# Index scores, turned rows and the mask moved beside the projection slabs of a two-layer decoder step

## The chip, the cores and the metric

The program runs on one core of one Trainium2 chip. The metric is the device time of one execution in microseconds (us), from launch to end, on that core. In the rows PE is TensorE's matmul side, PEld its weight loads, ACT ScalarE, DVE VectorE, POOL GpSimd, SP SyncE (it only issues transfers here); "ACTq" and "SPq" are the transfers that those engines issue.

## The reference, cut to what matters

One step of a decoder with two layers over 256 prompt tokens and 8 sample tokens (264 columns), width 2048, all in f32. Layer 0 picks keys with an indexer, layer 1 uses a forget gate. Both also attend into 256 memory tokens, and both end in a mixture of experts.

```python
# layer 0
q, k, v, qi, ki, wi, qm = split(h @ w_in)          # qi: 16 index heads of 64, ki: one index key
s = einsum('qhd,ld->qlh', qi, ki) * 64 ** -0.5
score = einsum('qlh,qh->ql', relu(s), wi * 16 ** -0.5)
sel = top_k(where(pos_k <= pos_q, score, -1e30), topk)   # prompt: 64 of 256; sample: 256 of 2049
# attention with ALiBi over the selected keys only
# layer 1
q, k, v, f, qm = split(h @ w_in)
c = cumsum(concat(cached log f, log_sigmoid(f + b_f)))   # bias c_q - c_k on the scores
# both layers
mk, mv = mem @ w_mem_kv                            # 256 memory tokens, 4 heads
mix = concat(self attention, memory attention) @ w_o
h = LN(alpha * h + mix); h = LN(alpha * h + moe(h))
```

The keys, values, index keys and forget gates of the sample tokens' past (8 sequences x 16 pages x 128 tokens) lie in pages that are found through a page table. New keys and values, memory keys and values, index keys and gates are outputs too.

## The kernel before, in words

Activations stand with the feature on the partition: `X` holds 16 chunks of 128 x 264 (`Xc`), `AT` the same for the memory tokens (`Ac`). Weights pass through a ring of six 2 MB slots (`ring`). `plan` lists the ring's units of each layer in order, SP issues them in that order, and a unit waits until the slot's last user has left it (`free`). PE waits for a unit with `arrived` and gives it back with `leave`.

A **slab** (`slab`, matmuls on L620) is one projection of 512 output columns: two units of 2 MB, 2 halves x 4 blocks f x 8 chunks c, so 64 f32 matmuls of 128x128 by 264 columns (128 records in the trace, since each f32 matmul is recorded twice). It fills four of the eight PSUM banks, banks 4 to 7 and 0 to 3 in turn, and ACT copies them out (L1361). `slab` has a hook, `beside(x)`: it is called after each four matmuls, x from 0 to 15, and what it issues stands between the slab's matmuls in PE's order. Before the change only layer 1's gates use it (`gate_sums`, L752; `gate_rows`).

The order on PE up to the attention, each step starting when the last is through:

- Layer 0, start: constants, page table, `ln` rows, the ALiBi table (1 MB) and then x are loaded. `turn_rows(0, "x")` transposes x (L596 for the 256 prompt rows, L598 for the 8 sample rows), and ACT copies it to `X`.
- `indexer`: the projection to index keys and head weights (`kiwi`, L659 and L661), a few transposes of it, two slabs `qi`. Then 16 prompt index steps (L689: PE two matmuls, ACT two Relus on L1421, DVE two multiply-adds on L1819/L1821). Then the cached index keys: 16 pieces are turned (L728), copied by ACT, multiplied with the queries (`product`, L705), rectified (L1430) and summed over heads (`rows`, L715). DVE then finds the 256 largest of 2049 per sequence (`sample_topk`, 32 pairs on L1803/L1804, ends with `mask_ready`), after that the prompt's 64 of 256 (`prompt_topk`), then waits in `add_mask` (L1874).
- Slabs q (3), kv, qm. Then `natural` (L640) turns new keys and values back to token rows for the outputs; ACT copies and stores them.
- `memory`: `turn_rows(layer, "mem")` transposes the memory tokens (L596) into `Ac`, two slabs `mkv`, `natural` for memory keys and values.
- Layer 0 only: `mask_rows` (L784) spreads the mask over partitions for `add_mask`. ACT's `pad_queries` puts the queries into two zeroed tiles `Qz`, `Qmz`, which POOL clears once `memory_done` is given after ACT's stores. `sample_scores` turns cached keys (L807) and multiplies (L816).
- Layer 1 is the same without the indexer, with 3 q, 2 kv and 1 qm slab. `cached_gates` (L777) turns the cached gates after `natural`; they were loaded by ACT in 128 small transfers.

ACT issues the page loads of the cached index keys for six sequences (`load_ik`), three before each of the two `qi` slabs are copied; SP loads the other two into the ring unit `ik`.

After this come attention, the output projection (L1066), the experts (L1227, L1257, L1271), untouched here.

## Time and profile before

| | |
|---|---|
| median of 3 runs | 2381.66 us (2380.25 to 2386.26) |
| the profiled execution's own time | 2382.95 us |
| its span, first to last instruction | 2381.3 us |
| PE busy | 2212.7 us, 93% |
| DVE busy | 669.0 us, 28% |
| ACT busy | 492.4 us, 21% |
| read from HBM | 640.20 MB, 271 GB/s over the span |
| mean granted TensorE clock | 0.963 of full |

The share of PE is an average over stages. To read the profile for this change one looks at the stretches in which PE is less than fully busy or at its lower clock, in the 378 us before layer 0's cached keys and between 1192 and 1462 us for layer 1, and asks in each what ended the waits.

### The profile page before, as it was taken

How to read it: one execution, taken by the hardware profiler on the slowest of the kernel's cores; microseconds unless marked ns; L12 is line 12 of the kernel's file. 1: busy time of each engine (PE TensorE's matmuls, PEld its weight loads, DVE VectorE, ACT ScalarE, POOL GpSimd, SP SyncE). 2: the span in 40 equal slices, each digit the busy share in tenths (PEclk: the TensorE clock that was granted, in tenths of full speed). 3: DMA queues.
4: the chain of work that ended last, by engine and by line, in shares of the span. 5: the costliest groups of instructions: out<-in, count | busy, mean ns of one | idle time of the engine just before them, and what ended most of it. 6: DMA issues, size and time to landing. Idle time of an engine off the chain costs nothing.

```text
span 2381.3 us, 32060 instructions
## 1 busy us (share of the span) xinstructions
PE 2212.7 (93%) x12475; PEld 1388.5 (58%) x12475; DVE 669.0 (28%) x1226; ACT 492.4 (21%) x1112; POOL 4.2 (0%) x10
## 2 busy tenths in 40 slices
PE   6989999999999999999899998999999999998996
PEld 4768886577863434343377876644778443443433
DVE  0059940421283121222410010023015622222124
ACT  1130015530140101010220023742103311010114
POOL 0000000000000000000000000000000000000000
PEclk9999999999989999999999998998999999999998
DMA  8714356794329999999944444998632599999992
GB/s 264 220 66 147 141 156 206 234 319 176 118 88 428 389 430 402 429 402 422 380 155 125 160 165 153 361 339 302 246 142 107 210 427 402 429 394 428 385 429 108
DMA packets 210148, 647.88 MB, mean 272 GB/s; under 512 B 56841, under 2 KB 90266, under 8 KB 184154
## 3 DMA queue, kind: packets, MB, share of 16 engines
q1 hardware_dynamic: 174650, 636.32, 69.3%
q10 hardware_dynamic: 35376, 9.91, 1.8%
q8 instruction: 80, 1.31, 0.2%
q14 instruction: 42, 0.34, 0.0%
HBM read 640.20 MB, written 5.96 MB: 271 GB/s over the span
## 4 chain that ended last, share of the span: by engine, by line
PE 75%; DMA 13%; ACTq 4%; DVE 3%; ACT 3%; issue 2%; SPq 0%; DVEq 0%
PE bank L620 17%; PE bank L1227 12%; PE bank L1066 9%; DMA ring<-in_w_down 8%; PE bank L1257 7%; PE bank L1271 5%; DMA ring<-in_w_up 4%; PE bank L807 4%; PE bank L1212 4%; ACTq L395 3%; PE bank L816 2%; PE bank L947 2%; ACT arena L1361 2%; PE bank L928 1%; PE bank L1119 1%
## 5 line engine op out<-in xcount | busy, mean ns | idle before, releaser
L1227 PE MATMUL bank<-ring,AT 128*64 128x512 f32 x2048 | 451.6, 599 | 24.3 <-DMA ring<-in_w_up 21.9
L1361 ACT ACTIVATE arena<-bank 128x512 f32<-128x512 f32 (+2 forms) x530 | 260.8, 541 | 995.3 <-PE bank L620 357.7
L620 PE MATMUL bank<-X,ring 128*128 128x264 f32 x1664 | 377.6, 390 | 11.3 <-ACT X L1593 7.3
L620 PEld LDWEIGHTS bank<-X,ring 128*128 128x128 f32 x1664 | 319.4, 192 | 68.5 <-issue 8.6
L1227 PEld LDWEIGHTS bank<-ring,AT 128*64 128x64 f32 x2048 | 146.9, 138 | 319.3 <-issue 285.9
L1257 PE MATMUL bank<-ring,arena 128*64 128x512 f32 x1024 | 238.4, 622 | 42.3 <-DMA ring<-in_w_down 35.0
L1066 PE MATMUL bank<-AT,ring 128*128 128x264 f32 x1024 | 237.7, 395 | 7.1 <-DVEq L1952 7.1
L1066 PEld LDWEIGHTS bank<-AT,ring 128*128 128x128 f32 x1024 | 199.6, 196 | 43.2 <-issue 7.9
L2228 DVE TENSOR_TENSOR X<-bank,X 128x264 f32<-128x264 f32 x256 | 110.8, 433 | 331.0 <-PE bank L1271 328.1
L1257 PEld LDWEIGHTS bank<-ring,arena 128*64 128x64 f32 x1024 | 77.9, 143 | 192.5 <-issue 167.1
L1271 PE MATMUL bank<-arena 128*128 128x264 f32 x512 | 118.2, 389 | 0.0
L807 PEld LDWEIGHTS bank<-consts,ring 128*128 128x128 f32 x768 | 86.9, 146 | 49.4 <-ACT arena L1361 34.9
L1271 PEld LDWEIGHTS bank<-arena 128*128 128x128 f32 x512 | 96.0, 190 | 28.6 <-ACT arena L1361 13.0
L620 PE MATMUL bank<-AT,ring 128*128 128x256 f32 x512 | 110.9, 379 | 0.0
L807 PE MATMUL bank<-consts,ring 128*128 128x128 f32 x768 | 101.1, 287 | 7.0 <-issue 4.4
L620 PEld LDWEIGHTS bank<-AT,ring 128*128 128x128 f32 x512 | 97.1, 190 | 13.1
L1361 ACT ACTIVATE AT<-bank 128x512 f32<-128x512 f32 (+3 forms) x136 | 60.9, 481 | 173.9 <-PE bank L1212 166.6
L1803 DVE MAX8 arena<-arena 8x8 f32<-8x2049 f32 (+1 forms) x48 | 79.9, 1664 | 28.9 <-ACT arena L1361 27.3
L1212 PE MATMUL bank<-arena 128*128 128x256 bf16 x768 | 86.6, 273 | 0.0
L1212 PEld LDWEIGHTS bank<-arena 128*128 128x128 bf16 x768 | 73.8, 98 | 11.8 <-issue 3.4
L1804 DVE MATCH_REPLACE8 arena<-arena 8x2049 f32<-8x2049 f32 (+1 forms) x48 | 79.1, 1647 | 0.0
L1662 ACT ACTIVATE arena<-bank 128x512 f32<-128x512 f32 x16 | 9.6, 598 | 290.5 <-PE bank L1227 290.5
(326 smaller groups left out, 1433.7 us busy)
## 6 DMA issues: line engine op xcount, KB each, us to landing
ring<-in_w_gate SPq DMA_DIRECT2D x64, 2048.0 KB, 17.2
ring<-in_w_up SPq DMA_DIRECT2D x64, 2048.0 KB, 14.0
ring<-in_w_down SPq DMA_DIRECT2D x64, 2048.0 KB, 16.7
ring<-in_w_o SPq DMA_DIRECT2D x16, 2048.0 KB, 10.5
ring<-in_cache_b_k SPq DMA_DIRECT2D x128, 256.0 KB, 4.2
ring<-in_cache_b_v SPq DMA_DIRECT2D x128, 256.0 KB, 4.7
ring<-in_w_in_a SPq DMA_DIRECT2D x14, 2048.0 KB, 9.3
ring<-in_w_in_b SPq DMA_DIRECT2D x12, 2048.0 KB, 11.2
```

The source lines that it names most:

```text
L395: eng.dma_start(dst(g + k), cache[bass.ds(page, 1)].rearrange("a p w -> (a p) w")).then_inc(sem, 16)
L620: mm = pe.matmul(B[4 * (g % 2) + f][:, 0:n_tok], u[:, c * 512 + f * P:c * 512 + (f + 1) * P], src[8 * half + c][:, 0:n_tok], start=(half = ...
L807: mm = pe.transpose(B[(4, 5, 7)[m % 3]][:, pg * P:(pg + 1) * P], tile[:, x:x + P], ident)
L1066: mm = pe.matmul(B[bank0 + f][:, 0:T], u[:, c * 512 + f * P:c * 512 + (f + 1) * P], Ac[8 * half + c], start=(half == 0 and c == 0), stop=( ...
L1212: mm = pe.matmul(B[banks[g]][:, c * 2 * P:(c + 1) * 2 * P], M.part[t][k][:, at:at + P], M.sel[:, t * 2 * P:(t + 1) * 2 * P], start=False, ...
L1227: mm = pe.matmul(B[bank][64 * s:64 * s + 64, :], M.xsT[:, at:at + 64], ring[slots[s][0]][:, c * FE:(c + 1) * FE], start=(half == 0 and c = ...
L1257: mm = pe.matmul(B[2 + q][64 * s:64 * s + 64, :], M.hT[:, at:at + 64], ring[slots[s][0]][:, j * D + q * 512:j * D + (q + 1) * 512], start= ...
L1271: pe.matmul(B[2 + c % 4][:, 0:T], M.ys[:, c * P:(c + 1) * P], M.gt[a], start=True, stop=True).then_inc(sm("scattered"), 1)
L1361: return act.activation(out, in_, ACT.Copy, scale=scale)
L1803: link(dve.max(m8, sc))
L1804: link(dve.match_replace(sc, m8, sc, TAKEN))
L2228: dve.tensor_tensor(Xc[c], B[2 + c % 4][:, 0:T], Xc[c], ALU.add).then_inc(sm("scatter_added"), 1)
```

## The change

- **Start.** x is loaded first, in four units of 512 columns of each token row (`x` 0 to 3); the identity (the first 128 columns of the constants) and the sample rows come with the first. The page table follows, then `kiwi` in one transfer of 80 columns, then `ln` with the rest of the constants and the small biases. ALiBi comes with the unit `q` 3. `turn_x` turns the sample rows in 16 transposes and each prompt chunk in 2.
- **Index projection.** 16 matmuls with 80 output rows in place of 32 matmuls. Its transposes, the `ln` transpose and the head-weight product stand beside slab `qi` 0 (`turn_keys`).
- **Index scores.** Prompt steps 0 to 7 (heads of the first `qi` slab, order `INDEX_STEPS`) beside `qi` 1, steps 8 to 15 and the whole work on cached index keys beside q 0 (`index`).
- **Page loads.** ACT issues sequences 0 to 2 before the first `qi` slab is copied, 3 and 4 in pieces of four pages between the prompt steps; SP issues sequences 5 to 7.
- **Rows.** The memory unit comes ahead of the last kv slab, and its transposes stand beside that slab. Key and value rows and (layer 1) cached gates are turned beside qm, memory keys and the mask's spread beside `mkv` 1. Only the memory values' `natural` stands alone.
- **Queries.** POOL clears `Qz` early and ACT fills it right after the qm slab; `Qmz` (it shares its space with the memory values) is filled after the 12th turned piece of `sample_scores`.

The diff, cut to its core (ACT's, DVE's and POOL's sides follow the same order):

```diff
@@ plan
-        u += [("ln", 0, 5), ("x", 0, 1), ("xs", 0, 1), ("kiwi", 0, 2), ("qi", 0, 1), ("qi", 1, 1), ("qi", 2, 1),
-              ("qi", 3, 1), ("ik", 0, 16 * (NB - IK_EARLY))]
+        u += [("x", 0, 3), ("x", 1, 1), ("x", 2, 1), ("x", 3, 1), ("kiwi", 0, 1), ("ln", 0, 4)]
+        u += [("qi", k, 1) for k in range(4)] + [("ik", 0, 16 * (NB - IK_EARLY))]
...
-    u += [("q", k, 1) for k in range(6)]
-    u += [("kv", k, 1) for k in range(2 if layer == 0 else 4)]
-    u += [("qm", k, 1) for k in range(2)]
-    u += [("mem", 0, 1)] + [("mkv", k, 1) for k in range(4)]
+    u += [("q", k, 2 if layer == 0 and k == 3 else 1) for k in range(6)]
+    if layer == 1:
+        u += [("kv", k, 1) for k in range(2)]
+    u += [("mem", 0, 1)] + [("kv", 2 * layer + k, 1) for k in range(2)]
+    u += [("qm", k, 1) for k in range(2)] + [("mkv", k, 1) for k in range(4)]
@@ gpsimd
+                    pool.wait_ge(S("ix_rows_copied"), 5)
...
+                pool.memset(a.Qz, 0.0).then_inc(S("zeroed"), 1)
                 pool.wait_ge(S("memory_done"), layer + 1)
-                pool.memset(a.Qz, 0.0).then_inc(S("zeroed"), 1)
                 pool.memset(a.Qmz, 0.0).then_inc(S("zeroed"), 1)
@@ tensor
+            def turn_chunk(t, width, at, bank=0):
+                n = bump("rows_turned")
+                if n > 4:
+                    pe.wait_ge(S("rows_copied"), n - 4)
+                for g in range(2):
+                    mm = pe.transpose(B[bank + n % 4][:, g * P:(g + 1) * P], t[:, g * width + at:g * width + at + P], ident)
+                mm.then_inc(S("rows_turned"), 1)
...
+            def turn_memory(layer, x):
+                if x == 1:
+                    pe.wait_ge(S("slab_copied"), cnt["slab"] - 1)
+                    arrived(pe, layer, "mem")
+                if 1 <= x <= 8:
+                    t = ring[units[layer]["mem", 0][0]]
+                    for c in (2 * x - 2, 2 * x - 1):
+                        turn_chunk(t, D, c * P, 4)
...
+            def memory_rows(layer, a, x):
+                if x == 2:
+                    pe.wait_ge(S("slab_copied"), cnt["slab"] - 1)
+                if x in (2, 3):
+                    natural(a.memK, HM, x - 2, SEQ)
+                if layer == 0:
+                    if x == 5:
+                        pe.wait_ge(S("natural_copied"), cnt["natural"])
+                        pe.wait_ge(S("mask_ready"), 1)
+                    if 5 <= x <= 8:
+                        pe.matmul(B[x - 5][:, :], cst("to12", NB), a.S[0:NB, 512 * (x - 5):512 * (x - 4)], start=True, stop=True)\
+                          .then_inc(S("mask_rows"), 1)
+                    if x == 12:
+                        pe.wait_ge(S("mask_added"), 1)
...
@@ indexer
+                    if 1 <= x <= 4:
+                        prompt_step(6 + 2 * x, 0)
+                        prompt_step(7 + 2 * x, 2)
...
+                    if 6 <= x <= 12 and x % 2 == 0:
+                        product(x // 2 - 3)
+                    if x == 12:
+                        new_key()
+                    if 7 <= x <= 13 and x % 2:
+                        rows((x - 7) // 2)
+                    if x == 14:
+                        rows(4)
+                    if 4 <= x <= 11:
+                        turn_cached(2 * x - 8)
+                        turn_cached(2 * x - 7)
+
+                pe.wait_ge(S("ixp_relu"), 8)
+                slab(0, "q", 0, Xc, T, index)
                 pe.wait_ge(S("ix_rows_copied"), 5)
@@ layers
-                slab(layer, "qm", 0, Xc, T)
-                slabs_done()
-                natural(a.kT, a.nk, 3)
-                natural(a.vT, a.nk, 3)
-                if layer == 1:
-                    cached_gates(a)
-                pe.wait_ge(S("natural_copied"), cnt["natural"])
+                slab(layer, "kv", layer, Xc, T, lambda x: turn_memory(layer, x))
+                pe.wait_ge(S("rows_copied"), cnt["rows_turned"])
+                slab(layer, "qm", 0, Xc, T, lambda x: own_rows(layer, a, x))
                 memory(layer, a)
-                if layer == 0:
-                    mask_rows(a)
```

How the change moves instructions is plainest in PE's order in layer 0. Before, the cached index keys are a stage of their own ahead of the q slabs (L728 turns, L705 is the product, L715 the sum over heads):

```order
103 L705 MATMUL bank<-arena 32x512 [waits kt_copied]
104 L705 MATMUL bank<-arena 32x512 x3
105 L728 MATMUL bank<-consts,arena 64x128 [waits kt_copied]
106 L728 MATMUL bank<-consts,arena 64x128 x7
107 L728 MATMUL bank<-consts,arena 64x128 [waits kt_copied]
108 L728 MATMUL bank<-consts,arena 64x128 x7
109 L715 MATMUL bank<-arena 8x512 [waits ix_relu]
```

Nothing of a slab stands between these rows: each `kt_copied` is a wait on ACT's copy of a piece turned just before.

PE in the change, at x = 5 to 7 of slab q 0 (L642 is the slab, L768 turns, L778 is the product, L796 the sum over heads):

```order
103 L642 MATMUL bank<-X,ring 128x264 x4
104 L768 MATMUL bank<-consts,arena 64x128 [waits kt_copied]
105 L768 MATMUL bank<-consts,arena 64x128 x7
106 L768 MATMUL bank<-consts,ring 64x128 [waits kt_copied]
107 L768 MATMUL bank<-consts,ring 64x128 x7
108 L642 MATMUL bank<-X,ring 128x264 x4
109 L778 MATMUL bank<-arena 32x512 [waits ixp_relu,kt_copied]
110 L778 MATMUL bank<-arena 32x512 x3
111 L768 MATMUL bank<-consts,arena 64x128 [waits kt_copied]
112 L768 MATMUL bank<-consts,arena 64x128 x7
113 L768 MATMUL bank<-consts,arena 64x128 [waits kt_copied]
114 L768 MATMUL bank<-consts,arena 64x128 x7
115 L642 MATMUL bank<-X,ring 128x264 x4
116 L796 MATMUL bank<-arena 8x512 [waits ix_relu]
```

Four slab matmuls now stand between the steps of the chain, and the same waits on ACT's copies are kept.

PE in the change, in slab `mkv` 1 of layer 0 (L658 is `natural`, L691 the mask's spread). Before, the spread stood behind both `mkv` slabs:

```order
234 L642 MATMUL bank<-AT,ring 128x256 x11
235 L658 MATMUL bank<-consts,arena 128x128 [waits natural_copied,slab_copied]
236 L658 MATMUL bank<-consts,arena 128x128 x3
237 L642 MATMUL bank<-AT,ring 128x256 x4
238 L658 MATMUL bank<-consts,arena 128x128 [waits natural_copied]
239 L658 MATMUL bank<-consts,arena 128x128 x3
240 L642 MATMUL bank<-AT,ring 128x256 x8
241 L691 MATMUL bank<-arena,consts 128x512 [waits mask_ready,natural_copied]
242 L642 MATMUL bank<-AT,ring 128x256 x4
```

PE now meets the wait for `mask_ready` 24 matmuls into that slab, where before it met it after the slab and the `natural` of all memory rows.

## Rows read from the trace of the kernel before

**Rows 1.** Stretches: us, busy us of PE, PEld, DVE, ACT, POOL; granted clock, DMA share, GB/s.

```profile
0.00:33.00 33.00, 14.32 (x52) 8.34 (x53) 0.02 (x1) 7.82 (x18) 0.41 (x5) 1.00 0.91 298
109.00:128.00 19.00, 12.66 (x69) 5.98 (x68) 12.80 (x27) 11.80 (x40) 0.00 (x0) 0.91 0.36 119
128.00:158.00 30.00, 25.27 (x307) 17.05 (x308) 2.53 (x7) 14.18 (x29) 0.00 (x0) 0.94 0.06 18
131.00:132.00 1.00, 1.00 (x14) 1.00 (x12) 0.00 (x0) 0.60 (x1) 0.00 (x0) 0.50 0.00 0
...
368.00:378.00 10.00, 7.68 (x29) 4.00 (x27) 0.00 (x0) 3.90 (x11) 1.42 (x2) 0.86 0.75 228
700.00:1192.00 492.00, 453.22 (x2370) 198.88 (x2366) 129.84 (x237) 64.66 (x122) 0.00 (x0) 0.97 0.98 405
1377.00:1393.00 16.00, 10.88 (x78) 7.82 (x77) 5.54 (x4) 11.18 (x30) 0.00 (x0) 1.00 0.58 200
1448.00:1462.00 14.00, 5.35 (x31) 4.41 (x31) 0.00 (x0) 5.03 (x15) 1.84 (x2) 0.71 0.67 225
```

**Rows 2.** Chain of waits from the start (start us, us, what).

```profile
8.35 10.16 DMA ring<-in_x_sample
18.64 0.66 PE bank L596 x2
...
32.97 9.33 PE bank L659 x32
42.30 7.24 PE bank L661 x32
```

**Rows 3.** DMA issues of 0 to 170 us (KB each, median us to landing).

```profile
consts<-in_consts SPq DMA_DIRECT2D x1, 1127.0 KB, 4.9
```

**Rows 4.** Timeline, the qi slabs (start us, us, engine).

```profile
51.91 57.20 PE L620 MATMUL bank<-X,ring 128*128 128x264 f32 x256 [0.38 <-ACT arena L1361]
...
53.79 27.89 ACTq L395 DMA_DIRECT2D arena<-in_cache_a_ik  x48
```

**Rows 5.** Chain of waits, index stage and q slabs of layer 0.

```profile
139.89 1.90 PE bank L728 x32
141.78 1.00 PE bank L705 x8
...
144.99 1.02 PE bank L715 x2
...
157.88 142.68 PE bank L620 x640
```

**Rows 6.** Timeline of DVE, top-k of layer 0.

```profile
157.92 2.28 DVE L1803 MAX8 arena<-arena 8x8 f32<-8x2049 f32 x1 [27.29 <-ACT arena L1361]
...
308.20 1.22 DVE L1830 TENSOR_SCALAR arena<-arena 8x2049 f32<-8x2049 f32 x1
...
327.09 0.43 DVE L1839 TENSOR_TENSOR arena<-arena,consts 128x256 f32<-128x256 f32 x1
```

**Rows 7.** Chain of waits, end of layer 0's projections.

```profile
313.08 55.28 PE bank L620 x256
...
372.90 4.92 PE bank L784 x8
378.04 4.75 PE bank L807 x24
...
383.78 1.93 PE bank L807 x16
```

**Rows 8.** Chain of waits in layer 1.

```profile
1214.93 3.76 PE bank L620 x16
...
1377.51 1.25 ACT arena L1361 x4
...
1392.77 55.28 PE bank L620 x256
...
1461.71 2.82 PE bank L807 x12
```

More of the change, by code:

```diff
@@ L68 @@
 IK_EARLY = 6
+INDEX_STEPS = [(t, c) for half in range(2) for t in range(2) for c in range(4 * half, 4 * half + 4)]
 CONST = {}
@@ L498, in _ @@
                         for b in range(n_seq):
-                            pages(layer, s, 4 * q + half + b, 4 * j, 4, ck,
+                            pages(full(layer, s), 4 * q + half + b, 4 * j, 4, ck,
                                   lambda g: t[:, (4 * b + g - 4 * j) * W:(4 * b + g - 4 * j + 1) * W])
@@ L503, in _ @@
                         b, first = divmod(k * per, PAGES)
-                        pages(layer, s, b, first, per, cv, lambda g: t[:, (g - first) * W:(g - first + 1) * W])
+                        pages(full(layer, s), b, first, per, cv, lambda g: t[:, (g - first) * W:(g - first + 1) * W])
                     elif name in ("mk", "mv"):
@@ new lines, in memory @@
+            def memory(layer, a):
+                pe.wait_ge(S("natural_copied"), cnt["natural"])
+                if layer == 1:
+                    pe.wait_ge(S("lf_copied"), 4)
+                slab(layer, "mkv", 0, Ac, SEQ)
+                slab(layer, "mkv", 1, Ac, SEQ, lambda x: memory_rows(layer, a, x))
+                pe.wait_ge(S("slab_copied"), cnt["slab"])
+                if layer == 0:
+                    pe.wait_ge(S("mask_added"), 5)
+                for t in range(2):
+                    natural(a.mvT, HM, t, SEQ)
@@ L1749, in _ @@
                 natural([(P, KN[:, 0, :]), (P, KN[:, 1, :]), (NB, a.KNs[:, 0:a.W])], a.W)
+                natural([(P, VN[:, 0, :]), (P, VN[:, 1, :]), (NB, a.VNs)], a.W)
+                if layer == 1:
+                    for j in range(4):
+                        act.wait_ge(S("lf_turned"), j + 1)
+                        copy(a.S[:, 512 * j:512 * j + 512], B[2 + j % 2][:, :]).then_inc(S("lf_copied"), 1)
                 act.wait_ge(S("natural_copied"), cnt["natural"])
```

425 lines of the change are left out of this document (216 added, 209 removed).

## The prediction

> **What bounds the kernel now.** I read the stretches first. The experts, 700 to 1192 us, are fed by memory [rows 1]: DMA share 0.98 at 405 GB/s, PE busy 453 of 492 us. This change leaves them alone, and their ring of six slots starts to fill only when the output projection gives slots back, so time saved ahead of them should shift them whole. Ahead of them PE is the bound, and in [rows 1] the reader is to look for stretches in which it is not full: the first 33 us (14.3 busy), the prompt index steps (12.7 of 19), the cached index keys (25.3 of 30, clock 0.94), 368 to 378, 1377 to 1393 (10.9 of 16) and 1448 to 1462 (5.4 of 14, clock 0.71). The chain of waits then says what each step costs PE, and the timelines say what the other engines need. A slab is 142.68 / 5 = 28.54 us of PE without a gap [rows 5], so 4 matmuls, the distance of two visits, last 1.78 us; a memory slab is 55.28 / 2 = 27.64 [rows 7], 0.432 per matmul. Work put between slab matmuls still costs its own PE time; what can be saved is waits and low clock.
>
> **The start.** Before, the sample rows (behind 1 MB of ALiBi, the constants and x) land at 8.35 + 10.16 = 18.5 us, turning takes until 32.97, the index projection until 49.5, and slab qi 0 starts at 51.9 [rows 2, 4]. In the change the first unit is 640 KB. The constants, 1127 KB and the very first transfer, landed 4.9 us after issue [rows 3]; with some 1.6 us of issuing ahead, PE can start at about 5 us (bounds 3.5 and 8). Turning is nearly the same PE work: 18.64 to 32.97 holds 16 chunks and two releases, 14.3 us, in which a pair of transposes takes 0.62 to 0.66. I take 13.3, as some gaps go; ACT's copies stay beside. The projection is 16 matmuls in place of 32: the first 16 took 9.33 us, the second 7.24 [rows 2]; I keep 9.3, the price of whoever comes first. That is 5 + 13.3 + 9.3 = 27.6 us. Ahead of and with qi 0 lie 5.9 MB, at 298 GB/s [rows 1] some 20 us plus 2, so the weights are there. **Gain so far 24.3 us.** Bounds: 18 (weights or x late) and 32.
>
> The level of the clock decides a part of this. The granted clock reads 1.00 here, but transposes of 0.31 us against 1.93 / 16 = 0.121 later [rows 2, 7] are at the lower, 1.2 GHz level, and PE left it only in the projection (9.33 against 7.24). The Trainium skill (TensorE: Matmul & The Clock Gate, "Part 1: The HAM clock gate") says that the throttled state is the default and that sustained activity releases it. The trace agrees for the projection and not for the turning, which kept the low level for 14 us.
>
> **Index keys, prompt steps, cached keys (layer 0).** Beside qi 0 go a handful of small transposes, 1.6 us (between 49.54 and 51.91 stood about that much work with two waits). The 16 prompt steps cost 12.66 / 16 = 0.79 us of PE each at most, partly at low clock, each matmul's modelled end included [rows 1]; in a dense stream I take 0.5 (half the bound, 0.4, is the other end). Eight stand beside qi 1: 4.0 us, and 0.4 for the wait on the last Relu ahead of q 0, because ACT issues four pages before each Relu: a page load costs it 27.89 / 48 = 0.58 us [rows 4], so 2.3 us and 0.7 for Relus, against 8 slab matmuls and a step, 4.1 us, between visits. ACT keeps pace. The 16 page issues before the kiwi copies take 9.3 us from about 18 and end at 28, 9 us before PE asks at x = 4. So q 0 starts at 27.6 + 1.6 + 57.2 + 4.0 + 0.4 = 90.8. Beside q 0: swap 0.3, eight steps 4.0, 16 turned pieces at 1.90 / 2 = 0.95, four products at 1.00, four head sums at 1.02, the new key 0.5 [rows 5]: 28.1 us. Each step waits for a copy that was started at least 1.78 us earlier and takes 0.6, so I see no wait of PE. SP issues 48 pages instead of 32 before q 0's weights, some 34 us from 28; q 0 is wanted at 90.8. q 0 ends at 90.8 + 28.5 + 28.1 = 147.4, before 157.88 + 28.5 = 186.4. **Gain 39.0.**
>
> **Rows of memory, keys and values.** Four more slabs are 114.2; beside them 32 memory transposes (3.9) and 12 of keys and values (1.5) at 0.121: 267.0. The stage between 300.56 and 313.08 is gone. `mkv` 0: 294.6. `mkv` 1 carries 8 transposes (1.0) and the mask's spread, four matmuls like the 1.02 us head sum (4.1; the 4.92 of [rows 7] is partly at low clock), 0.2 for the last column: 327.5. Behind it stay the slab's copies and one `natural`, 2.9 us with ACT's lag (bounds 1.5 and 6, the latter if stores get in the way): 330.4, against 378.04. **Gain 47.6**, and 4.75 - 24 x 0.121 = 1.9 more if the clock no longer falls ahead of the scores [rows 7]: 49.5.
>
> The cover is thin in one place. DVE needs 308.20 + 1.22 - 157.92 = 151.5 us from the last index row to `mask_ready`, and 169.6 until it can add the mask [rows 6]. It now starts at about 145.6, so it is ready at 297.1 and 315.2. PE asks 24 matmuls into `mkv` 1, at 294.6 + 10.4 + 1.0 = 306.0, and for the first added block 28 matmuls and the spread later, at 322.2. Spare: 9 and 7 us. If the cover is gone, PE stands still inside `mkv` 1, and the next late thing is the mask's last column.
>
> **Layer 1.** The stage from 1377.51 to 1392.77 [rows 8], 15.3 us, goes, and its 72 transposes (24 key and value, 16 gate, 32 memory) cost 8.7 beside the slabs: 6.5. From the end of `mkv` 1 (1448.05) to the fourth turned piece (1461.71) pass 13.7 us, with PE busy 5.4: ACT stores, waits for POOL's clearing and then for its own stores. Now `natural` and three pieces (1.5) with ACT's lag are 4.4, and memory keys' transposes cost 1.0 inside the slab: 8.3. The pieces behind start at low clock (2.82 for 12 transposes, not 1.45), with the product after them some 2.0. Sum 16.8. POOL's clearing of `Qmz` (under 1.5 us) has eleven pieces of cover; without it PE would wait at the first memory score only.
>
> **What a visit costs.** The order shows 68 visits to slabs in both layers. After the gate projection of layer 1, 16 slab records took 3.76 us [rows 8] instead of 16 x 0.223 = 3.57: 0.19 us for the return. From turns to product there is none (139.89 + 1.90 = 141.79, [rows 5]). Bounds 0 and 68 x 0.19 = 13; I take 5, nearer the transposes, which most visits are.
>
> The Trainium skill (same page, "Architectural detail: the array is 16× 32×32, not 1× 128×128") says that PE pulls weight loads ahead of matmuls in flight; by it a return is free and the sum is 5 us better, 2316. The 0.19 us after the gates says not always.
>
> **Sum.** 49.5 + 16.8 - 5 = 61.3 us. Against the profiled execution's 2382.95 that is 2321.7; the median shown is 1.3 lower, so I say 2321.
>
> **The rivals.**
> - *Full clock from early on.* Turning without the single 8-column transposes in between is denser, and leaves the low level sooner: 32 x (0.31 - 0.12) = 6.1 and 9.33 - 7.24 = 2.1 on the projection, so 2313. Against: the turning before did not. By the Trainium skill's rule above it is the normal case. 12%.
> - *Visits are dear.* 0.19 each (8 us more) and prompt steps at 0.79 (4.6 more): 2334. For: the return after the gates. 12%.
> - *Late start.* x in pieces, `kiwi` in 320-byte rows and ACT's page loads share the engines, and qi 0 starts 10 us later: 2331. For: DMA share 0.91 in the first 33 us. 8%.
> - *The gain doesn't pass on*, or the top-k runs over its spare: 10 to 15 us back, 2334. 5%.
> - *The clock falls in the mixed slabs.* Small matmuls and short waits between slab matmuls make PE look idle; at 131 us, right behind the prompt steps, the granted clock is 0.50, that is 1.2 GHz [rows 1]. The nine slabs with visits hold about 308 us of PE work, and work at the lower level takes twice as long: 61 us of it eat the gain, 68 make the kernel slower by over 0.3%, and a third of it (103) gives 2425. Against: the cached keys themselves, 25.3 of 30 us busy, kept 0.94, and slabs are denser. 3%.
>
> **How the numbers follow.** The forecast holds 60%, the rivals 12, 12, 8, 5 and 3. The range 2307 to 2342 takes in all but the last, with the bounds of start (18 to 32), visits (0 to 13) and steps. A measurement of this kernel can tell about 0.3%, 7 us, from no change. All cases but the last are faster by more: faster 0.96, same 0.01, slower 0.03.
>
> **What would show it.** Right: qi 0 at 25 to 31 us, q 0 about 57 us long and free of waits, the first max of the top-k near 146, layer 0's turned keys from about 330, layer 1's stages of 15 and 14 us gone but for 4, experts unchanged. Wrong: PE waiting for DVE inside `mkv` 1, a granted clock under 0.9 in a mixed slab, qi 0's weights landing after 30, or experts longer than before by what was saved.

## The result and the profile after

| | before | changed |
|---|---|---|
| median of 4 runs each | 2380.99 us (2380.25 to 2386.26) | 2315.35 us (2314.17 to 2321.91) |
| ratio, 95% interval | | 0.9725 [0.9702, 0.9748] |
| the profiled execution's own time | 2382.95 us | 2314.92 us |
| its span | 2381.3 us | 2313.1 us |
| PE busy | 2212.7 us, 93% | 2181.2 us, 94% |
| mean granted clock | 0.963 | 0.973 |

Forecast was 2321 us with a range of 2307 to 2342. The two profiled executions lie 68.0 us apart, where the sum said 61.3. PE is busy 31.5 us less although its work has hardly changed: the projection to index keys has 16 matmuls fewer (7.3 us), and most of the rest is, as the mean granted clock of 0.973 against 0.963 suggests, work that now runs at the higher clock. The other half of the 68 us is waiting that is gone.

The stretches of the kernel after, in the columns of [rows 1]:

```profile
0.00:24.00 24.00, 17.01 (x87) 13.01 (x88) 0.02 (x1) 7.54 (x19) 0.41 (x5) 1.00 0.90 292
57.00:86.00 29.00, 29.00 (x134) 21.29 (x132) 6.39 (x14) 4.60 (x14) 0.00 (x0) 1.00 0.87 282
118.00:148.00 30.00, 30.00 (x251) 20.28 (x248) 1.18 (x1) 9.75 (x18) 0.53 (x1) 1.00 0.18 63
...
653.00:1144.00 491.00, 451.71 (x2369) 200.73 (x2364) 129.29 (x237) 64.29 (x121) 0.00 (x0) 0.98 0.98 406
1320.00:1336.00 16.00, 16.00 (x82) 13.73 (x81) 4.59 (x3) 2.98 (x5) 0.00 (x0) 1.00 0.84 309
1392.00:1399.00 7.00, 5.13 (x42) 3.60 (x41) 0.00 (x0) 5.34 (x12) 0.95 (x1) 1.00 0.64 198
```

Prompt steps (57 to 86) and cached index keys (118 to 148) now stand among slab matmuls: PE is full, at a clock of 1.00, where before these stages had 12.7 of 19 and 25.3 of 30 us [rows 1]. The experts read as before, DMA share 0.98 at 406 GB/s. The 15 us stage of layer 1 is part of a full slab (1320 to 1336), and of the 14 us behind `mkv` 1 six are left, with 1.00 instead of 0.71. The first experts matmul comes at 649.78 us instead of 697.10, layer 1's first slab at 1144.51 instead of 1192.19: what was saved ahead of the experts passed through them. That it did so to 0.1 us is luck of this pair: the same untouched stretch differs by up to 4 us between other traces (table below).

The timeline of PE at the start (start us, us, engine, line, tiles; idle before and its releaser in brackets) answers to [rows 2, 4]:

```profile
6.18 1.87 PE L613 MATMUL bank<-consts,ring 8*128 8x8 f32 x16 [6.18 <-DMA ring<-in_x_prompt]
7.98 1.97 PE L604 MATMUL bank<-consts,ring 128*128 128x128 f32 x8
...
14.03 1.09 PE L604 MATMUL bank<-consts,ring 128*128 128x128 f32 x8
15.06 0.20 PE L597 MATMUL bank<-consts 32*32 32x32 f32 x1
15.19 7.35 PE L716 MATMUL bank<-X,ring 128*80 128x264 f32 x32
23.35 6.94 PE L642 MATMUL bank<-X,ring 128*128 128x264 f32 x30 [0.82 <-DMA ring<-in_w_in_a]
```

Eight transposes take 1.97 us at first and 1.09 us from 14.03: the clock rose during the turning. The granted clock reads 1.00 for all of 0 to 24 us; at the start the durations tell the level, not that column. The projection then runs at the rate that [rows 2] show only for its second half. In front of slab `qi` 0 PE waits 0.82 us for weights, and SP's timeline says why they come late:

```profile
3.99 0.37 SPq L447 DMA_DIRECT2D ring<-in_w_in_a  x1
4.40 5.77 SPq L470 DMA_DIRECT2D ring<-in_ln_g  x1
...
13.96 12.02 SPq L447 DMA_DIRECT2D ring<-in_w_in_a  x4
```

SP stands 5.77 us in the issue behind that of `kiwi`, and nine more loads follow (one of them, the rest of the constants, of 1063 KB) before the slab's weights are issued at 13.96.

The timeline of PE in `mkv` 1 of layer 0, and DVE's of the same stretch, answer to [rows 6, 7]:

```profile
302.84 3.62 PE L642 MATMUL bank<-AT,ring 128*128 128x256 f32 x16
306.38 1.12 PE L691 MATMUL bank<-arena,consts 8*128 8x512 f32 x2
307.44 1.99 PE L642 MATMUL bank<-AT,ring 128*128 128x256 f32 x8
...
316.36 7.17 PE L642 MATMUL bank<-AT,ring 128*128 128x256 f32 x32
323.46 0.38 PE L695 MATMUL bank<-arena,consts 8*128 8x1 f32 x2
...
331.45 1.47 PE L876 MATMUL bank<-consts,ring 128*128 128x128 f32 x12
333.57 1.63 PE L876 MATMUL bank<-consts,ring 128*128 128x128 f32 x12 [0.65 <-ACT arena L1421]
```

```profile
146.82 2.28 DVE L1878 MAX8 arena<-arena 8x8 f32<-8x2049 f32 x1 [41.28 <-ACT arena L1421]
...
297.10 1.22 DVE L1904 TENSOR_SCALAR arena<-arena 8x2049 f32<-8x2049 f32 x1
```

The mask is ready at 298.3 and asked for at 306.4: 8 us to spare, and no wait at either place. Behind that, 8 records of the slab take 1.99 on the timeline where 16 take 3.62, so one visit costs the slab matmuls that follow about 0.2 us.

Layer 1's waits sit in two places. First PE behind `mkv` 1:

```profile
1393.45 1.09 PE L658 MATMUL bank<-consts,arena 128*128 128x128 f32 x8 [1.30 <-ACT arena L1421]
```

and then inside slab q 1 and in front of q 2, which the change doesn't touch:

```profile
1194.73 0.31 PE L852 MATMUL bank<-consts,arena 12*128 12x12 f32 x3 [1.51 <-ACT arena L1421]
...
1213.60 16.73 PE L642 MATMUL bank<-X,ring 128*128 128x264 f32 x74 [3.77 <-ACT arena L1421]
```

ACT's own timeline has the cause: it issues 31 loads of cached gates in one go while PE waits for copies that stand behind them on ACT.

```profile
1194.75 18.43 ACTq L398 DMA_DIRECT2D arena<-in_cache_b_lf  x31
```

### The profile page after: what moved, and what is told of

The parts are those of the page before. It is cut to its first block, busy times and chain, and to the rows that moved or that the text cites. A ratio compares the mean times of both kernels' runs of the same rounds, so it can differ in the third digit from the quotient of the medians.

```text
span 2313.1 us, 32005 instructions
## 1 busy us (share of the span) xinstructions
PE 2181.2 (94%) x12445; PEld 1369.2 (59%) x12445; DVE 669.1 (29%) x1226; ACT 494.5 (21%) x1115; POOL 4.3 (0%) x10
## 4 chain that ended last, share of the span: by engine, by line
PE 74%; DMA 14%; SPq 5%; DVE 2%; issue 2%; ACTq 1%; ACT 1%; DVEq 0%
PE bank L642 20%; PE bank L1296 13%; PE bank L1135 9%; DMA ring<-in_w_down 8%; PE bank L1326 7%; PE bank L1340 5%; DMA ring<-in_w_up 4%; PE bank L1281 4%; SPq L398 3%; PE bank L876 3%; PE bank L1016 1%; PE bank L886 1%; ACTq L398 1%; PE bank L1188 1%; PE bank L768 1%
## 5 line engine op out<-in xcount | busy, mean ns | idle before, releaser
L1296 PE MATMUL bank<-ring,AT 128*64 128x512 f32 x2048 | 452.1, 599 | 25.1 <-DMA ring<-in_w_up 23.3
L1421 ACT ACTIVATE arena<-bank 128x512 f32<-128x512 f32 (+5 forms) x531 | 262.2, 541 | 877.8 <-PE bank L642 264.0
L642 PE MATMUL bank<-X,ring 128*128 128x264 f32 x1664 | 387.3, 390 | 11.9 <-ACT X L1671 7.3
L642 PEld LDWEIGHTS bank<-X,ring 128*128 128x128 f32 x1664 | 312.9, 191 | 71.1 <-issue 14.5
L1326 PE MATMUL bank<-ring,arena 128*64 128x512 f32 x1024 | 233.7, 612 | 44.0 <-DMA ring<-in_w_down 38.7
L1340 PEld LDWEIGHTS bank<-arena 128*128 128x128 f32 x512 | 96.0, 190 | 28.6 <-ACT arena L1421 13.0
L642 PE MATMUL bank<-AT,ring 128*128 128x256 f32 x512 | 112.8, 380 | 0.0
L876 PEld LDWEIGHTS bank<-consts,ring 128*128 128x128 f32 x768 | 82.1, 140 | 42.9 <-ACT arena L1421 34.4
L642 PEld LDWEIGHTS bank<-AT,ring 128*128 128x128 f32 x512 | 96.6, 190 | 15.8 <-issue 3.0
L876 PE MATMUL bank<-consts,ring 128*128 128x128 f32 x768 | 96.4, 278 | 1.2 <-ACT arena L1421 1.2
L1281 PEld LDWEIGHTS bank<-arena 128*128 128x128 bf16 x768 | 73.9, 98 | 11.6 <-issue 3.4
## 6 DMA issues: line engine op xcount, KB each, us to landing
ring<-in_w_o SPq DMA_DIRECT2D x16, 2048.0 KB, 11.3
```

What stands on the lines that cost most here:

```text
L642: mm = pe.matmul(B[4 * (g % 2) + f][:, 0:n_tok], u[:, c * 512 + f * P:c * 512 + (f + 1) * P], src[8 * half + c][:, 0:n_tok], start=(half = ...
L876: mm = pe.transpose(B[(4, 5, 7)[m % 3]][:, pg * P:(pg + 1) * P], tile[:, x:x + P], ident)
L1281: mm = pe.matmul(B[banks[g]][:, c * 2 * P:(c + 1) * 2 * P], M.part[t][k][:, at:at + P], M.sel[:, t * 2 * P:(t + 1) * 2 * P], start=False, ...
L1296: mm = pe.matmul(B[bank][64 * s:64 * s + 64, :], M.xsT[:, at:at + 64], ring[slots[s][0]][:, c * FE:(c + 1) * FE], start=(half == 0 and c = ...
L1326: mm = pe.matmul(B[2 + q][64 * s:64 * s + 64, :], M.hT[:, at:at + 64], ring[slots[s][0]][:, j * D + q * 512:j * D + (q + 1) * 512], start= ...
L1340: pe.matmul(B[2 + c % 4][:, 0:T], M.ys[:, c * P:(c + 1) * P], M.gt[a], start=True, stop=True).then_inc(sm("scattered"), 1)
```

## The experiments

"Undone" means that one part of the changed kernel was put back and all else left. "Given back" compares medians with the changed kernel's 2315.35 us. The 95% interval of each single part undone overlaps that of the change, so each size is also read in the traces. The table cuts each span at four points on PE: the start of `qi` 0, the first product of layer 0's sample scores (L886), layer 1's first slab, and the first such product there.

| us | to `qi` 0 | to product, layer 0 | attention and experts | layer 1 to product | rest |
|---|---|---|---|---|---|
| before | 51.9 | 330.8 | 809.5 | 272.3 | 916.8 |
| changed | 23.4 | 311.8 | 809.4 | 253.5 | 915.1 |
| index work ahead | 22.9 | 321.1 | 805.5 | 251.9 | 915.7 |
| rows ahead | 23.0 | 317.9 | 806.1 | 258.8 | 915.6 |
| old loads | 28.6 | 311.7 | 809.1 | 251.6 | 918.3 |
| queries late | 24.4 | 314.3 | 806.7 | 257.3 | 917.9 |
| all four | 28.5 | 328.2 | 805.6 | 260.6 | 918.3 |

The third and the last column hold work that no edit touches, and still they differ by 4 and 3 us. A difference of a few us between two whole times therefore shows little here; the place where it arises does.

### Four parts undone

**Index work ahead of its slabs.** `apart` makes `slab` call `beside(x)` for all x first, and then issue its matmuls bare.

```diff
+                if apart:
+                    for x in range(16):
+                        beside(x)
+                    beside = None
...
-                slab(0, "qi", 1, Xc, T, first_heads)
+                slab(0, "qi", 1, Xc, T, first_heads, apart=True)
-                slab(0, "q", 0, Xc, T, index)
+                slab(0, "q", 0, Xc, T, index, apart=True)
```

> The changed kernel, but prompt steps 0 to 7 stand ahead of slab qi 1 and steps 8 to 15 with all cached index keys ahead of slab q 0, in their old dense order; ACT's page loads of sequences 3 and 4 come behind the first eight Relus. Theory (the stage was long because PE waited on ACT and DVE between its steps, and slab matmuls fill these waits): the two stages take about 50 us of which PE needs 38 beside the slabs, so 12 to 16 us slower than the changed kernel, 2327 to 2331 us, with PE idle in both stages and the granted clock falling behind the first. Rival (visits cost PE nearly as much as the waits did): within 5 us of the changed kernel.

Measured 2322.75 us (2318.8 to 2329.49), ratio 0.9763 [0.9732, 0.9794]: 7.4 us given back, where 12 to 16 were expected from the waits and at most 5 by the rival. From the end of `qi` 0 to the end of q 0 it takes 104.0 instead of 94.7 us, 9.3 more; the whole span grew by less since the untouched attention and experts were 3.9 us shorter in this trace and PE's waits in layer 1's gates 2.0. PE's waits in the two index stages are back, 11.3 us in all instead of 0.4, four of them of 0.7 us like this one:

```profile
111.87 1.06 PE L782 MATMUL bank<-arena 128*32 128x512 f32 x8 [0.70 <-ACT arena L1425]
112.87 1.97 PE L772 MATMUL bank<-consts,arena 128*64 128x128 f32 x32
```

The granted clock also fell, to 0.66 from 94 to 99 us. That 11 us of waits and a lower clock make only 9.3 fits what the undone kernel doesn't pay: the 23 visits to these two slabs have a return of 0.2 us each (below), 4.6 us.

**Rows ahead of their slabs.** The same for kv and qm of both layers and `mkv` 1 of layer 1.

```diff
-                slab(layer, "qm", 0, Xc, T, lambda x: own_rows(layer, a, x))
+                slab(layer, "qm", 0, Xc, T, lambda x: own_rows(layer, a, x), apart=True)
```

> The changed kernel, but the transposes of memory, keys, values and cached gates (both layers) and of layer 1's memory keys stand ahead of their slab instead of between its matmuls. Theory (ACT's copies of 0.4 to 0.6 us pace them, against 0.11 us per transpose beside a slab): memory 4 us more in each layer, own rows 3 and 4 us more, memory keys 1.5: 16 us slower than the changed kernel, 2331 us (2326 to 2337). Rival (the earlier memory unit and the lack of waits for POOL and the stores made the gain, not the cover): 2 to 5 us slower.

Measured 2324.16 us (2322.13 to 2325.39), ratio 0.9759 [0.9731, 0.9787]: 8.8 us given back, half of what was expected, in the trace 12.7: by ACT's copies the stages grow by 2.2 (kv) and 3.9 (qm) in layer 0 and 2.2, 2.9 and 1.5 in layer 1. Against that the untouched stretch was 3.2 us shorter and the gate waits 1.8. PE's waits on ACT in the pieces that were moved are 7.7 us, eight of them, the longest 1.4: I had taken ACT to be late at every piece, and it mostly isn't.

**Old order of the first loads.** The rest of the constants and ALiBi ahead of x; page table, `kiwi` and `ln` stay behind it.

```diff
+            sp.dma_start(consts[:, P:], i["consts"][:, P:]).then_inc(S("consts_in"), 16)
+            sp.dma_start(lay[0].S[NB:P, 0:L1], i["alibi"][NB:P, :]).then_inc(S("alibi_in"), 16)
             pregs = [sp.alloc_register(f"page{k}") for k in range(8)]
```

> The changed kernel, but all constants and ALiBi are loaded ahead of x again (page table and kiwi stay behind x). Theory (PE's start is set by the first x unit, and qi 0 by turning and projection): 2 MB more ahead of x are 5 to 6 us at about 385 GB/s, PE starts at 12 instead of 6.2, and the whole run is 6 us slower, 2321. Rival (the start is bound by the bytes ahead of slab qi 0, and PE's turning has slack): only ALiBi is new ahead of qi 0, 2.7 us, 2318.

Measured 2320.96 us (2311.67 to 2322.2), ratio 0.9734 [0.97, 0.9769]: +5.6, but the interval holds the changed kernel's 0.9725, so the times alone show nothing. The trace is clear: PE begins at 13.16 instead of 6.18, `qi` 0 at 28.63 instead of 23.35, and from there to the first product of layer 0 both take the same (311.7 and 311.8). That is 5.3 us, near the theory's 6 and not the rival's 2.7.

**Queries padded at the old place.** `pad_queries` behind `memory_done`.

```diff
-                pad_queries(layer, a)
...
                 act.sem_inc(S("memory_done"), 1)
+                pad_queries(layer, a)
```

> The changed kernel, but POOL clears Qz only behind memory_done and ACT fills it then, as before. Theory: three turned pieces go ahead, then the first product waits for POOL's 0.5 (layer 0) and 1.0 us (layer 1) and ACT's two or four fills of 0.2 us, and ACT's copies of turned pieces queue behind them: 2 us in layer 0, 3 in layer 1, 5 us slower, 2320. Rival (the first pieces turned cover it): no change within 1 us.

Measured 2318.86 us (2314.55 to 2322.53), ratio 0.9731 [0.9702, 0.976]. The interval holds 0.9725 here too. In the trace PE waits 3.5 us for ACT in front of its turned keys (L876), in two waits, instead of 1.2: the part is worth 2.3 us, between the theory's 5 and the rival's 1. The rest of what this trace has more is not the queries: `qi` 0 began 1.1 us later, behind 3.15 us of waiting for weights, and ran its first matmuls at a granted clock of 0.77, which cost 1.7; in layer 1 the clock fell behind the gate wait.

**All four at once.**

> The changed kernel with the four parts undone together that were undone one by one: work beside qi 1 and q 0 issued ahead of those slabs, work beside kv, qm and layer 1's mkv 1 likewise, the old order of the first loads, queries padded at the old place. Left in place: x in pieces as first unit of weights, sample rows in 16 transposes, 16 projection matmuls, small transposes beside qi 0, layer 0's mkv 1 with its visits, ACT's page loads. Theory A (the parts stand at different places of PE's one chain and add): +7.4 + 8.8 + 5.6 + 3.5 = +25.3 over the changed kernel, 2340 to 2342 us; so 40 of the 66 us come from what is left in place. Theory B (parts overlap: with the late start ACT's page loads and the weights are early, so waits that each part alone laid open are hidden): 2332 to 2336.

Measured 2341.89 us (2339.23 to 2342.88), ratio 0.9823 [0.9793, 0.9853]. By the medians that is +26.5 where the four single steps add to 25.3, by the ratios +23.3; the theory that they add was 2340 to 2342, the rival 2332 to 2336. The traces bear out the sum piece by piece: the start is 5.2 us later (old loads alone 5.3), layer 0 from `qi` 0 to its product takes 16.4 more (9.3, 6.1 and 0.9 alone), layer 1 takes 7.1 more (rows alone 5.3, queries 1.4). The parts stand at different places of one chain and don't cover for one another.

So some 39 of the 66 us come from what was left in. This kernel's span is 40.2 us shorter than that of before: 23.4 stand at the start (`qi` 0 at 28.50, before at 51.91), 2.7 more up to the first product of layer 0 (356.65, before 382.72), 11.7 in layer 1, and 2.4 in stretches that no edit touched. Of the 23.4 at the start, 5.5 are that PE begins earlier (13.13 and 18.64), 5.9 that turning takes 8.2 instead of 14.1, and 12.0 lie between turning and `qi` 0: 7.3 for the 16 projection matmuls that are gone, 2.3 for the others at the higher clock, 2.4 for the small stage now beside `qi` 0.

### The thin cover of the mask

Six more passes of `max` over the index rows make `mask_ready` 14 us later.

```diff
                 top_k(sc, a.m8[0:NB, :], TOPK_S)
+                for _ in range(6):
+                    link(dve.max(a.m8[0:NB, :], sc))
```

> The changed kernel with six idle max searches of 2.3 us, 13.9 us of DVE, between the last pair of the sample top-k and mask_ready. In the changed kernel mask_ready is given at 298.3 us and PE asks at 306.4 (8 us of cover); the first added block is asked for at 323.5 and ready at 317.1 (6 us). Theory (the cover is what the two clocks say): PE waits 5.8 us ahead of the first spread in slab mkv 1, 1.5 to 2 us more ahead of the last column, 7 to 8 us slower, 2323 us. Rival (the waits are hidden further on by the k units or ACT): no change. Rival (the whole DVE chain is on the path): 14 us slower.

One run, 2330.4 us; the kernel before took 2391.55 beside it, more than in its other runs, so the whole time decides nothing between the theory's 2323 and the rival's 14 us more. The same holds for the two kernels of the next section: what they show is read in their traces. PE's timeline in `mkv` 1:

```profile
306.21 3.62 PE L642 MATMUL bank<-AT,ring 128*128 128x256 f32 x16
315.74 2.04 PE L691 MATMUL bank<-arena,consts 8*128 8x512 f32 x2 [5.91 <-DVE arena L1906]
317.71 3.78 PE L642 MATMUL bank<-AT,ring 128*128 128x256 f32 x8
321.42 1.46 PE L691 MATMUL bank<-arena,consts 8*128 8x512 f32 x2
322.81 1.99 PE L642 MATMUL bank<-AT,ring 128*128 128x256 f32 x8
```

The wait is 5.91 us, at the place and near the size that the cover of 8 us gives (13.9 of extra work less 8). But the slab takes 43.0 instead of 34.0 us: behind the wait the two records of one matmul take 2.04 instead of 1.12 and eight records 3.78 instead of 1.99, the lower clock. A wait of 6 us cost 9. The span grew by 15.5: 3.4 more were lost at `qi` 0, which waited 3.46 us for its weights and then ran at the lower clock, 2.4 in layer 1, the rest in stretches that no edit touches.

### What a visit costs

Each prompt step beside `qi` 1 split over two visits, one matmul in each:

```diff
-                    if x % 2 and x < 14 or x == 14:
-                        prompt_step(x // 2, 4 + 2 * (x // 2 % 2))
+                    prompt_half(x // 2, 4 + 2 * (x // 2 % 2), x % 2)
```

> The changed kernel, but each of the eight prompt steps beside slab qi 1 is split into its two matmuls, one per visit: 16 visits instead of 8. In the changed kernel a visit with one step takes 0.63 us and one with two steps 1.06, so 0.43 a step, and 8 slab records behind it 1.98 instead of 1.78. Theory (0.2 us on entry and 0.2 on return, whatever the visit holds): each visit with one matmul takes about 0.4 and the return 0.2, slab qi 1 is 8 x 0.4 = 3.2 us longer. Rival (only the return costs): 1.6 us longer. Rival (the 0.2 belongs to each matmul, not to the visit): no longer than now.

One run, 2327.68 us; from the end of `qi` 0 to that of q 0 it takes 7.35 us more, where 3.2 were expected (1.6 and 0 by the rivals). Two lines of PE's timeline, of this kernel and then of the changed one:

```profile
60.05 0.70 PE L753 MATMUL bank<-arena 64*128 64x256 f32 x2
60.67 2.05 PE L642 MATMUL bank<-X,ring 128*128 128x264 f32 x8
```

```profile
83.62 0.70 PE L745 MATMUL bank<-arena 64*128 64x256 f32 x4
84.25 2.05 PE L642 MATMUL bank<-X,ring 128*128 128x264 f32 x8
```

A visit with one matmul (two records) lasts 0.63 from start to start, and so does one with both. The two matmuls of a step have 64 input rows each, in different halves of the array, and here they cost no more than one. The eight records behind a visit take 1.98 us instead of 8 x 0.223 = 1.78 in both kernels: that is the return, 0.2 us. So eight more visits cost 8 x (0.63 + 0.2) = 6.6 us, and a wait of 0.75 for ACT in front of q 0 is the rest of the 7.35. Two steps in one visit, as beside q 0 of the changed kernel, take 1.07: a step itself is 0.43, and another 0.2 is paid on the way in.

Is the return due to the visit or to what runs in it? Memory's transposes as plain matmuls with the identity:

```diff
+                    if bank == 4:
+                        mm = pe.matmul(B[bank + n % 4][:, g * P:(g + 1) * P], t[:, g * width + at:g * width + at + P], ident,
+                                       start=True, stop=True)
+                        continue
                     mm = pe.transpose(B[bank + n % 4][:, g * P:(g + 1) * P], t[:, g * width + at:g * width + at + P], ident)
```

> The changed kernel, but the 32 memory chunks of each layer are turned by plain f32 matmuls against the identity, full 128x128 tiles, in place of transposes. In the changed kernel four transposes beside slab kv take 0.44 us and the 8 slab records behind them 1.78, with no return cost. Theory A (the return cost goes with another tile shape than the slab's): four matmuls of two records at 0.11 take 0.88 us and the records behind them stay at 1.78. Theory B (it goes with f32 matmuls as against transposes): 8 slab records behind a visit take 1.98. Either way 3.6 us more per layer for the second pass, under B 1.6 more: 2322 under A, 2326 under B.

One run, 2318.41 us, each kv slab 3.64 us longer. First this kernel, then the changed one:

```profile
208.60 1.05 PE L605 MATMUL bank<-consts,ring 128*128 128x128 f32 x8
209.49 1.95 PE L646 MATMUL bank<-X,ring 128*128 128x264 f32 x8
```

```profile
208.86 0.60 PE L604 MATMUL bank<-consts,ring 128*128 128x128 f32 x4
209.30 1.95 PE L642 MATMUL bank<-X,ring 128*128 128x264 f32 x8
```

Matmuls of full 128 x 128 tiles have no return either: the eight records behind them last 1.79 from start to start, as behind transposes. That is theory A, though the whole time lies below both its 2322 and B's 2326. So it is not matmuls as such that cost 0.2. The visits that pay had operands of 64 or 8 input rows, or of 64, 32 or 8 output rows (steps, mask, product, head sum). In most of them turned index pieces (matmuls with 64 output rows) stand beside the others, but in one visit to q 0 they stand alone, and the return is there too, 1.97 us from start to start behind them:

```profile
103.54 1.97 PE L768 MATMUL bank<-consts,arena 128*64 128x128 f32 x32 [0.42 <-ACT arena L1474]
105.44 2.05 PE L642 MATMUL bank<-X,ring 128*128 128x264 f32 x8
107.41 1.09 PE L768 MATMUL bank<-consts,arena 128*64 128x128 f32 x16
```

Transposes of sample rows, with only 8 output rows, have none (1.78 behind them in layer 1). So a small tile goes with the return in matmuls and not in transposes; why isn't settled.

### A version that beats both

**Gates alone.** ACT copies the gate rows of layer 1 ahead of most page loads.

```diff
                 for k in range(3):
-                    if layer == 1:
-                        load_lf(range(2 * k, 2 * k + 2))
                     if layer == 1 and k == 1:
                         gate_rows(a)
+                    if layer == 1:
+                        load_lf((range(0, 1), range(1, 4), range(4, 6))[k])
```

> The changed kernel with the gate edit alone (gate rows copied ahead of the page loads, one, three, two and two sequences). Theory: the two waits of 1.5 and 3.8 us go, 2310 us. Rival (ACT is late with slab copies instead): within 1 us of the changed kernel.

Measured 2309.14 us (2302.04 to 2312.64), ratio 0.9682 [0.9664, 0.97]. Both waits of layer 1 are gone. With 5.3 us of waits off the chain, 6.2 came back in the medians and 5.7 in layer 1 of the trace; the intervals of the two ratios end side by side (0.9702 and 0.97), so that it is faster is shown, the size is not certain: the same two waits are only 3.1 to 3.5 us in four of the kernels above, all with the gate code of the change. The rival, waits that only move to the kv slabs, is out: PE has none there.

**Four edits.** The same, the rest of the constants and the five loads of biases behind unit `qi` 1, prompt steps two to a visit, and the mask's spread in one visit:

```diff
-                    if x % 2 and x < 14 or x == 14:
-                        prompt_step(x // 2, 4 + 2 * (x // 2 % 2))
+                    if x in (2, 6, 10, 14):
+                        prompt_step(x // 2 - 1, 4)
+                        prompt_step(x // 2, 6)
...
-                    if 5 <= x <= 8:
+                    if x == 5:
+                        for j in range(4):
```

> The changed kernel with four edits. Layer 1: ACT copies the gate rows ahead of the page loads of cached gates, and issues one, three, two and two sequences around the slabs instead of two each time; the waits of 1.5 and 3.8 us in slabs q 0 to q 2 go (5.3 us). Start: the constants' rest and biases are loaded behind qi 1's first weights, slab qi 0 no longer waits 0.8 us. Prompt steps in pairs, four visits instead of eight, at 0.4 us each (1.6). The mask's spread in one visit instead of four (3 x 0.4, 1.2, less the cover of 3 us that PE asks sooner). Sum 8.9: 2306.5 us, 2304 to 2310. Rival (the gate waits only move to the kv slabs, where ACT is late with copies): 2312.

Measured 2302.74 us (2302.11 to 2305.11), ratio 0.9666 [0.9652, 0.9679]. `qi` 0 begins at 21.29 without a wait; its weights are issued at 11.64 instead of 13.96, still behind one issue of 5.81 us. Two edits gave less than expected. A pair does cost 1.25 instead of twice 0.83, but two Relus then end behind the slab, and PE waits 0.78 in front of q 0. And `mkv` 1 takes 34.5 us, not less than 34.0. Its stretches behind the spread, in the columns of [rows 1]:

```profile
303.60:307.30 3.70, 3.70 (x9) 1.40 (x8) 3.42 (x11) 0.00 (x0) 0.00 (x0) 1.00 0.34 114
307.30:310.00 2.70, 2.70 (x9) 2.27 (x9) 2.50 (x9) 0.00 (x0) 0.00 (x0) 0.66 0.00 0
310.00:313.00 3.00, 3.00 (x12) 2.46 (x12) 2.79 (x10) 0.00 (x0) 0.00 (x0) 0.74 0.00 0
```

PE was not idle by this profile, and yet the granted clock fell, behind four matmuls in a row with 8 input rows each.

**The spread back in four visits**, pairs one visit earlier, x in (1, 5, 9, 13):

> The version with later small loads, gate rows ahead of the page loads and prompt steps in pairs, but the mask's spread again in four visits, and the pairs one visit earlier (x = 1, 5, 9, 13). Theory A (four spreads in one visit, 3.7 us of matmuls with 8 input rows, made the granted clock fall behind them, 0.66 to 0.74 over 6 us; four visits kept it at 1.00): mkv 1 takes 34.0 rather than 34.5 us and shows a granted clock of 1.00 at 300 to 325 us; the wait of 0.78 us on ACT in front of q 0 goes, so index slabs take 93.2 to 93.6 us rather than 94.2; in all 1.0 to 1.5 us better than the version before it, 2301.5. Theory B (the clock behind the spread is chance or set by the stretch before): mkv 1 is again above 34.3 us or again shows a granted clock below 0.9 behind the mask rows, and the time is 2302 to 2303.

Measured 2303.98 us (2300.89 to 2311.71), ratio 0.9677 [0.9649, 0.9705]. `mkv` 1 takes 34.0 us and the clock stays:

```profile
304.60:313.00 8.40, 8.40 (x30) 5.19 (x30) 7.81 (x26) 0.00 (x0) 0.00 (x0) 1.00 0.20 56
```

From the end of `qi` 0 to the end of q 0 PE takes 93.1 instead of 94.1 us, and the wait of 0.78 is gone. In the traces both edits work as theory A has it, and the span is 1.2 us shorter (2299.1 and 2300.3); in the medians the two versions can't be told apart. One profile of each stands behind the reading of the clock, so that the row of spreads caused the fall is likely and not shown. Both are some 12 us faster than the change and 77 to 78 faster than before.

## Why the prediction was right, and where its terms were off

The direction and the size came out; the sum was 6.7 us short. By its own steps:

| step | predicted | measured |
|---|---|---|
| PE starts | 5 | 6.2 |
| turning x | 13.3 | 9.0 |
| index projection | 9.3 | 7.35, then 0.82 of wait |
| `qi` 0 begins | 27.6 (gain 24.3) | 23.35 (28.6) |
| `qi` 0 to the end of q 0 | 119.8 | 125.2 |
| q 0 ends | 147.4 (gain 39.0) | 148.5 (38.1) |
| `mkv` 1 ends | 327.5 | 329.2 |
| first product of layer 0 | gain 49.5, less visits | 47.6 |
| layer 1 | gain 16.8, less visits | 20.2 |

- **The start: mis-sized, and only in part by the clock.** "Turning is nearly the same PE work ... I take 13.3" was the step that failed: it took 9.0. PE's timeline before shows chunks alternate with 8-column transposes, 0.82 us from chunk to chunk, 0.20 of it for the 8 columns:

```profile
19.43 0.69 PE L596 MATMUL bank<-consts,ring 128*128 128x128 f32 x2
20.05 0.27 PE L598 MATMUL bank<-consts,ring 8*128 8x8 f32 x1
20.25 0.69 PE L596 MATMUL bank<-consts,ring 128*128 128x128 f32 x2
```

In the changed kernel four chunks take 1.90 at the same low level, 0.475 each, and the sixteen 8-column transposes in a row 1.80, 0.11 each. So at the low level alone the new order would take 10.0 us: of the 4.3 us, 3.3 go with no longer alternating two shapes, a term that I had at nothing, and 1.0 with the high level at the end. "I keep 9.3" for the projection was off by the clock, 7.35. What in the old turning held the clock low, the single 8-column transposes in between or something else, and what of the 3.3 us they cost, wasn't tried alone.

The first rival, full clock from early on, was right for the projection, and its 2313 is nearer than my 2321; but of the 6.1 us that it gave the turning 4.3 came, and most of these by the shapes and not by the clock. That its number comes so near is in part luck. By 14.0 us turning had left the low level in this trace, by 11.1, 11.6 and 11.9 in three kernels with the same turning. The Trainium skill (TensorE: Matmul & The Clock Gate, "Part 1: The HAM clock gate") lets sustained activity release the throttled state; these traces agree, with eight transposes at 1.97 us and then 1.09.
- **Weights for `qi` 0: "so the weights are there" was wrong**, by 0.8 us here and by 3.15, 3.26 and 3.46 in three kernels with the same first loads; behind each of these three the granted clock was 0.77 for 7.5 us, another 1.7 us. I summed bytes and left out the issuing: 5.77 us in one issue and nine behind it. With six of the nine moved the wait is gone. They hold 1.1 MB as well as six issues, and which of the two mattered wasn't separated.
- **Prompt steps: mis-sized.** I took 0.5 each; alone in a visit one costs 0.63, two in a visit 1.07. That is 9.3 instead of 8.0 us for 16; the 2.4 us of their returns belong to the next term.
- **Visits: right in their sum.** 0.2 us behind about 30 visits, none behind transposes, is 6; I took 5. The Trainium skill (same page, "Architectural detail: the array is 16× 32×32, not 1× 128×128") has weight loads pulled ahead of matmuls in flight, and taken at its word a return would be free; behind 128 x 128 tiles that agrees, behind steps, mask and sums it doesn't (1.98 against 1.78).
- **The cover of DVE: right.** 8 us to spare, 9 predicted; taken away, PE stood where it was said to. Dearer than said, since the clock falls with it.
- **Layer 1: right in its parts, and 2.0 us of luck.** Visits and pieces beside slabs gained 6.2 (6.5 predicted), the stage behind `mkv` 1 with the product at full clock 12.0 (8.3 and 2.0). Another 2.0 I had no term for. In both kernels PE waits for gate rows (3.31 before, 3.77 after), and behind it the clock fell in one of the two. The stretch right behind the wait, before, after, and in the kernel with more visits, which has the changed kernel's code there and a wait of 3.65:

```profile
1260.50:1268.00 7.50, 7.45 (x21) 5.95 (x22) 0.00 (x0) 1.24 (x4) 0.00 (x0) 0.63 0.72 213
```

```profile
1213.60:1221.00 7.40, 7.40 (x33) 6.36 (x34) 0.00 (x0) 1.24 (x4) 0.00 (x0) 1.00 0.70 199
```

```profile
1220.20:1227.70 7.50, 7.49 (x22) 6.01 (x23) 0.00 (x0) 1.24 (x4) 0.00 (x0) 0.64 0.68 197
```

The clock fell in the same way behind this wait in the three other kernels that have it at 3.27 to 3.73 us (granted clock 0.62, 0.66 and 0.77). Of all nine waits of 3.15 to 3.77 us in this place and in front of `qi` 0, it fell behind eight; the changed kernel's own is the exception. So these 2.0 us are luck of that execution, and I can't say what decides it. Behind the waits of 0.3 to 1.6 us in the same two places it stayed at 1.00.

- **The gain passes on: right.** 47.6 us ahead of the attention, 47.7 behind the experts; by other traces such a comparison is good to 4 us.
- **The clock falling in mixed slabs: didn't happen** in the changed kernel. That it can was seen in the version with four spreads in a row.

What stays open: of the 39 us that no step undid, 23 are seen at the start. The traces say where they lie, but x in pieces, fewer projection matmuls and the earlier clock were not taken out one by one.

## What to carry to other kernels

Where PE is the bound, steps that alternate with another engine belong between the matmuls of a projection that has nothing to wait for; what comes back is their waits and the clock those waits cost, while their own PE time stays. Price such a visit by its shape (here no return behind 128 x 128 tiles, 0.2 us behind smaller matmuls and about as much on the way in), put matmuls that use different parts of the array in one visit, and look at the clock behind several with few input rows in a row. Group transposes of one shape instead of alternating two (read from the traces, not tried alone). Then look at what the queues issue ahead of the first weights, and at which copies stand behind a run of page loads on the same engine.

## What the runs showed of the hardware

- One SP issue took 5.77 us, directly behind a transfer of 80 columns a row; 5.57 to 6.57 in the other kernels with the same order, 10.9 in the two with 2 MB more ahead of x, 0.3 to 0.5 for most other issues. Why it stalls wasn't tried.
- Two matmuls on 64 input rows each, in different halves of the array, took 0.63 us together, and one alone took 0.63.
- At the low clock level, a pair of 128-column transposes and one 8-column transpose in turn took 0.82 us; in groups of one shape they took 0.475 and 0.11.
- A granted clock of 0.66 to 0.74 over 5.7 us, behind 3.7 us of matmuls with 8 input rows, without any idle time; at 1.00 when slab matmuls stood between them (one profile each).
- A wait of 5.91 us halved the rate of the next 5 us of work; behind eight of nine waits of 3.15 to 3.77 us the granted clock read 0.62 to 0.77 over 7.5 us, behind the ninth 1.00.
- The same untouched 809 us of attention and experts took 805.5 to 809.5 us in the traces of these kernels.
